# Both half-step FFNs of a decoder trunk: the gate/up products of the last two steps side by side, three down products behind them, and every step's rows turned by DMA

## The reference, cut to what matters

```python
def swiglu(x, w_gate, w_up, w_down):
    return (jax.nn.silu(x @ w_gate) * (x @ w_up)) @ w_down

def reference(x, ...):
    for l in range(DEPTH):                                     # DEPTH = 2
        x = x + HALF_STEP * swiglu(rmsnorm(x, norm_ffn1[l]), w1_gate[l], w1_up[l], w1_down[l])
        h = rmsnorm(x, norm_mix[l])
        proj = h @ w_in[l]
        ...                        # differential attention and retention on proj
        x = x + mixed @ w_out[l]
        x = x + HALF_STEP * swiglu(rmsnorm(x, norm_ffn2[l]), w2_gate[l], w2_up[l], w2_down[l])
    return rmsnorm(x, norm_final)
```

## Time and profile before

| | us |
|---|---|
| median of 3 runs | 959.06 (958.98 to 961.36) |
| the profiled execution | 961.72 |
| its span, first to last instruction | 959.6 |
| PE busy | 948.7 (99%) |
| DVE / ACT / POOL busy | 557.2 / 459.6 / 203.0 |
| mean granted PE clock | 0.996 of full speed |

### The profile page before, as it was taken

One profiled execution on the slowest core, in us unless ns is written; L12 is line 12 of the kernel. 1 busy time (PEld: TensorE's weight loads), 2 busy tenths in 40 slices (PEclk: granted clock), 3 DMA queues, 4 the chain that ended last, 5 costly groups with the idle time before them and its releaser, 6 DMA issues.

```text
span 959.6 us, 12597 instructions
## 1 busy us (share of the span) xinstructions
PE 948.7 (99%) x4379; PEld 785.6 (82%) x4379; DVE 557.2 (58%) x623; ACT 459.6 (48%) x580; POOL 203.0 (21%) x237
## 2 busy tenths in 40 slices
PE   8999999999999999999999999999999999999997
PEld 7888888888888888888888888888888887888885
DVE  5555555666575555555666455556665756555554
ACT  6454444455564454444445444444657445444442
POOL 4433221000010442131023221210002024312110
PEclk9999999999999999999999999999999999999999
DMA  7788676735353877676737767664624647867651
GB/s 266 237 219 251 185 226 196 247 121 170 113 187 121 230 230 232 190 229 194 246 117 216 242 196 228 189 220 150 228 80 176 219 119 207 266 191 220 195 161 44
DMA packets 166051, 185.98 MB, mean 194 GB/s; under 512 B 49264, under 2 KB 139424, under 8 KB 166016
## 3 DMA queue, kind: packets, MB, share of 16 engines
q1 hardware_dynamic: 122080, 174.09, 54.8%
q10 hardware_dynamic: 43616, 10.52, 6.2%
q0 software_dynamic: 320, 0.92, 0.6%
HBM read 173.96 MB, written 1.05 MB: 182 GB/s over the span
## 4 chain that ended last, share of the span: by engine, by line
PE 95%; DVE 1%; ACT 1%; DMA 1%; POOL 1%; issue 0%; POOLq 0%; DVEq 0%; ACTq 0%
PE gu L871 20%; PE gu L873 20%; PE gu L872 20%; PE acc L871 10%; PE acc L873 10%; PE acc L872 10%; PE tp L889 1%; PE tp L1007 1%; DMA kT<-kT 1%; PE acc L1018 1%; PE tp L1030 1%; ACT w_hi L360 1%; DVE w_lo L596 0%; PE gu L1119 0%; ACT rT L397 0%
## 5 line engine op out<-in xcount | busy, mean ns | idle before, releaser
L596 DVE TENSOR_TENSOR w_lo<-raw,w_hi 128x2048 fp32r<-128x2048 f32 (+1 forms) x164 | 374.3, 2286 | 157.7 <-ACT w_hi L360 157.7
L871 PE MATMUL gu<-w_hi,xT_hi 128*128 128x512 f32 x892 | 350.4, 393 | 1.2 <-DVE w_lo L605 1.0
L873 PE MATMUL gu<-w_hi,xT_lo 128*128 128x512 f32 x892 | 347.9, 390 | 0.0
L872 PE MATMUL gu<-w_lo,xT_hi 128*128 128x512 f32 x892 | 347.4, 390 | 0.0
L360 ACT ACTIVATE w_hi<-raw 128x2048 fp32r<-128x2048 f32 (+1 forms) x164 | 305.5, 1866 | 14.5 <-DMA raw<-in_w_in_dram 7.2
L871 PEld LDWEIGHTS gu<-w_hi,xT_hi 128*128 128x128 f32 x892 | 167.7, 188 | 37.0 <-DVE w_lo L605 1.4
L873 PEld LDWEIGHTS gu<-w_hi,xT_lo 128*128 128x128 f32 x892 | 167.6, 188 | 35.3
L872 PEld LDWEIGHTS gu<-w_lo,xT_hi 128*128 128x128 f32 x892 | 167.7, 188 | 33.6
L871 PE MATMUL acc<-w_hi,aT_hi 128*128 128x512 f32 x384 | 150.8, 393 | 0.7 <-DVE aT_lo L625 0.7
L873 PE MATMUL acc<-w_hi,aT_lo 128*128 128x512 f32 x384 | 149.7, 390 | 0.0
L872 PE MATMUL acc<-w_lo,aT_hi 128*128 128x512 f32 x384 | 149.5, 389 | 0.0
(11 more groups left out here) (129 smaller groups left out, 433.6 us busy)
## 6 DMA issues: line engine op xcount, KB each, us to landing
raw<-in_w_down_dram SPq DMA_DIRECT2D x88, 512.0 KB, 4.1
raw<-in_w_gate_dram SPq DMA_DIRECT2D x84, 512.0 KB, 4.0
raw<-in_w_up_dram SPq DMA_DIRECT2D x84, 512.0 KB, 5.0
raw<-in_w_in_dram SPq DMA_DIRECT2D x40, 512.0 KB, 4.7
raw<-in_w_out_dram SPq DMA_DIRECT2D x16, 512.0 KB, 4.1
raw<-in_w_in_dram SPq DMA_DIRECT2D x16, 256.0 KB, 3.0
raw<-in_w_gate_dram SPq DMA_DIRECT2D x8, 256.0 KB, 4.0
raw<-in_w_up_dram SPq DMA_DIRECT2D x8, 256.0 KB, 4.6
```

What stands on the lines that cost most here:

```text
L596: nc.vector.tensor_tensor(w_lo[:, pos % SLOTS, 0:n], raw[:, pos % RAW, 0:n], w_hi[:, pos % SLOTS, 0:n].bitcast(F32), ALU.subtract).then_in ...
L871: nc.tensor.matmul(out_, s_hi, m_hi, start=first, stop=False)
L872: nc.tensor.matmul(out_, s_hi, m_lo, start=False, stop=False)
L873: return nc.tensor.matmul(out_, s_lo, m_hi, start=False, stop=last)
```

## The change

The last two steps change places with their down products. PE now does, behind the loop: gate/up of step 8; down of step 7; gate/up of step 9; gate/up of step 10; down of step 8; down of step 9, tile 0; down of step 10, tile 0; down of step 9, tile 1; `enter_T`; down of step 10, tile 1. The 16 transposes of hidden rows on PE are gone, step 10 is turned by DMA like the others. The loop has one round less (steps 2 to 7), steps 8 and 9 are written out. Since aT_hi and aT_lo hold two steps, step 10 overwrites what step 8 left: ACT waits for PE's down of step 8, tile 0 (`aT_read`) and tile 1 (`slot_free`) first. The splits of pieces 33 and 34 stand each one place later. SP loads the pieces in PE's new order.

```diff
-LOOPED = (STEPS - 3) // 2
+LOOPED = (STEPS - 5) // 2
...
# SP
-                e = FFN_PIECES - 4
-                load_gu(0, e, STEPS - 1)
-                load_down(0, e + 2, STEPS - 2)
-                load_down(0, e + 3, STEPS - 1)
+                e = FFN_PIECES - 10
+                load_gu(0, e, STEPS - 3)
+                load_down(0, e + 2, STEPS - 4)
+                load_gu(0, e + 3, STEPS - 2)
+                load_gu(0, e + 5, STEPS - 1)
+                for n in range(3):
+                    load_down(0, e + 7 + n, STEPS - 3 + n)
...
# POOL
-                with pool.Fori(1 if i else 5, STEPS - 1) as s_:
-                    step(2 * s_ + d0, 2 * s_ + e0)
+                with pool.Fori(1 if i else 5, STEPS) as s_:
+                    step(2 * s_ + e0, 2 * s_ + e0)
...
# ACT
-                def last_step(s_, par, it, pos, nxt):
-
-                    silu(s_, 0, it, pos)
+                def last_step(s_, d, par, pos, nxt):
+
+                    silu(s_, 0, 0, pos)
                     nxt(0)
-                    silu(s_, 1, it, pos)
-                    last_hi(par, 0)
+                    turn(d, 0)
+                    silu(s_, 1, 0, pos)
+                    turn(d + 1, 1)
+                    act.wait_ge(aT_read, i + 1)
+                    turned_hi(d, par, 0)
                     nxt(1)
-                    last_hi(par, 1)
+                    act.wait_ge(slot_free, SLOTS + LP * layer + base + FFN_PIECES - 2)
+                    turned_hi(d + 1, par, 1)
+                    nxt(2)
...
                 def last_lots(i):
                     if i == 0:
                         split_hi(layer, base + FFN_PIECES - 1)
-                        ahead_after(layer, f, [0])
-                    elif i == 1:
-                        ahead_after(layer, f, [1])
+                    else:
+                        ahead_after(layer, f, [i - 1])
...
-                last_step(s0 + STEPS - 1, 0, 0, FFN_PIECES - 3, last_lots)
+                e, s = FFN_PIECES - 10, STEPS - 3
+                step(s0 + s, d0 + 2 * s, 0, 0, e + 1, pieces(0, e + 3, e + 4, e + 5))
+                split_hi(layer, base + e + 6)
+                step(s0 + s + 1, d0 + 2 * s + 2, 1, 0, e + 4, pieces(0, None, e + 7, e + 8))
+                last_step(s0 + s + 2, d0 + 2 * s + 4, 0, e + 6, last_lots)
...
# DVE, last_step (last_lots and the calls change as on ACT)
                     hide(e, 0, d - 1)
                     nxt(0)
                     hide(e + 1, 1, d)
-                    last_lo(par, 0)
+                    turned_lo(d, par, 0)
                     nxt(1)
-                    last_lo(par, 1)
+                    turned_lo(d + 1, par, 1)
+                    nxt(2)
...
# PE
-                for tt in range(TT):
-                    if tt == 0:
-                        hidden_T(e, 0)
-                    down((dT_lo_done, d0 + 2 * (STEPS - 1) - 1 + tt), 0, p_ + 2, 1, tt)
-                    if tt == 0:
-                        hidden_T(e + 1, 1)
-                    if tt and f == 0:
...
+                for s in (1, 2):
+                    for tt in range(TT):
+                        up(e0 + n + 2 * s + tt, 0, p_ + 1 + 2 * s, tt)
+                down((dT_lo_done, d0 + n + 1), 0, p_ + 7, 0, 0).then_inc(aT_read, 1)
+                down((dT_lo_done, d0 + n + 2), 0, p_ + 7, 0, 1)
+                for tt in range(TT):
+                    down((dT_lo_done, d0 + n + 3 + tt), 0, p_ + 8, 1, tt)
+                    if tt and (f == 0 or layer < DEPTH - 1):
                         enter_T(q + 1, 0)
-                    down((hT_lo_done, 2 * i + tt + 1), 0, p_ + 3, 0, tt, last=True)
+                    down((dT_lo_done, d0 + n + 5 + tt), 0, p_ + 9, 0, tt, last=True)
```

More of the change, by code:

```diff
@@ L141, in build @@
         rstd_tmp, normed = sem("rstd_tmp"), sem("normed")
-        gu_ready, silu_done, hidden_done, hT_psum, hT_hi_done, hT_lo_done = (
-            sem(n) for n in ("gu_ready", "silu_done", "hidden_done", "hT_psum", "hT_hi_done", "hT_lo_done"))
+        gu_ready, silu_done, hidden_done, aT_read = (sem(n) for n in ("gu_ready", "silu_done", "hidden_done", "aT_read"))
         pool_seen, halves_seen = sem("pool_seen"), sem("halves_seen")
@@ L674, in turned_lo @@
                           aT_hi[:, ks, tt * P:(tt + 1) * P], dT_lo_done)
[L676 to L680, removed]
                 def step(e, d, par, it, nxt, guard=True):
@@ L717, in ffn @@
                         step(e0 + 4 * it + 4 + 2 * u, d0 + 4 * it + 4 + 2 * u, u, it, pieces(it, p_, p_ + 1, p_ + 2))
-                last_step(e0 + 2 * (STEPS - 1), d0 + 2 * (STEPS - 1), 0, last_lots)
+                e, n = FFN_PIECES - 10, 2 * (STEPS - 3)
+                step(e0 + n, d0 + n, 0, 0, pieces(0, e + 3, e + 4, e + 5))
+                split_lo(layer, base + e + 6)
+                step(e0 + n + 2, d0 + n + 2, 1, 0, pieces(0, None, e + 7, e + 8))
+                last_step(e0 + n + 4, d0 + n + 4, 0, last_lots)
             def mixer(layer):
@@ L954, in up @@
                     project(layer, it, tt, base + pos, 2, gu_ready, hook, entry, entry is not None and base == 0)
[L956 to L960, removed]
                 def down(ready, it, pos, par, tt, **kw):
                     pe.wait_ge(*ready)
-                    add_rows(layer, it, tt, base + pos, aT_hi, aT_lo, 2 * par, **kw)
+                    return add_rows(layer, it, tt, base + pos, aT_hi, aT_lo, 2 * par, **kw)
                 up(e0, 0, 0, 0, lambda: enter_T(q, 1), guard=False, entry=q)
@@ L978, in ffn @@
                             down((dT_lo_done, d0 + n - 1 + tt), it, 7 + 3 * u, 1 - u, tt)
-                e, p_ = e0 + 2 * (STEPS - 1), FFN_PIECES - 4
+                n, p_ = 2 * (STEPS - 3), FFN_PIECES - 10
                 for tt in range(TT):
-                    up(e + tt, 0, p_, tt)
+                    up(e0 + n + tt, 0, p_, tt)
                 for tt in range(TT):
-                    if tt == 0:
-                        hidden_T(e, 0)
-                    down((dT_lo_done, d0 + 2 * (STEPS - 1) - 1 + tt), 0, p_ + 2, 1, tt)
-                    if tt == 0:
-                        hidden_T(e + 1, 1)
-                    if tt and f == 0:
+                    down((dT_lo_done, d0 + n - 1 + tt), 0, p_ + 2, 1, tt)
+                for s in (1, 2):
[6 more added lines that the diff above has]
+                    if tt and (f == 0 or layer < DEPTH - 1):
                         enter_T(q + 1, 0)
-                    elif tt:
-                        if layer < DEPTH - 1:
-                            enter_T(q + 1, 0)
-                    down((hT_lo_done, 2 * i + tt + 1), 0, p_ + 3, 0, tt, last=True)
+                    down((dT_lo_done, d0 + n + 5 + tt), 0, p_ + 9, 0, tt, last=True)
             def mixer(layer):
```

15 lines of the change are left out of this document (6 added, 9 removed).

## The result

The changed kernel takes 969.11 us (median of 6 runs, 967.39 to 971.0) against 960.2 us for the kernel before in 6 runs beside it (958.98 to 961.36). The ratio is 1.0096, 95% interval 1.0086 to 1.0106: slower by 9.2 us, where 5.7 were forecast. The time lies inside the range of 958.0 to 969.5, at its upper edge, and 0.1 us above the 962.1 to 969 of the forecast case; the amount is 1.6 times what was forecast. The profiled execution took 969.58 us, its span is 967.8 us, 8.2 more than before.

A forecast was written before the change was run, and what follows sets the result against it. PE, busy 948.7 of 959.6 us, was taken to bound the kernel. Three ends waiting 2.6 us (7.8) less 2.1 us saved at four ends gave +5.7 us: 964.8 us, range 958.0 to 969.5.

The forecast's parts named there:

- the forecast case: PE waits 1.7 to 4.0 us at three FFN ends, giving 962.1 to 969 us; chance 0.57.
- a wait of 2.6 us an end: PE's two waits at each of three FFN ends: 0.8 us before the down block, 1.8 before enter_T.
- x: Time from issue of step 10's first turn to its copy back: taken as 6.7 us, with ends 2.56 and 8.1.
- the fall of the clock: Rival: PE's gaps slow one down block after the waits, 2.9 us an end, 973 or so; 0.11 shared with the second hold-up.
- The gain: Two pairs of transposes per FFN leave PE: 0.52 us an end, 2.1 us over four ends.
- The held copy: POOL's copy of step 10's first hidden rows takes 2.50 us beside DVE's w_lo; turn issued 2.85 us after w_lo began.
- the row of 7.20: Before's turn at the second FFN's start, issue to copy back, two loads issued 3.0 and 0.4 us earlier: 7.20 us.
- The row of 7.93: Before's turn at the same place in layer 1: 7.93 us to landing alone, so about 8.1 to the copy back.
- The clock on which step 10 was laid: Before's timeline reused for the new order: PE starts step 10's row tile 1 at 171.87, DVE w_lo of piece 31 at 172.03.
- The formula: Both PE waits together at an FFN end: x - 4.1 us, nothing below x = 4.1.
- The hidden turn: Rival: step 10's first turn is hidden after all, deciding at x = 5.8; 956.9 to 960.2 us; hidden or nearly so 0.28.
- The second hold-up: Rival: step 9's tile 1 copy back held beside w_lo, 2.72 us, +6 us more, 970 or so; 0.11 shared with the clock.

The follow-up runs named there:

- the kernel without transposes: Kernel before with the stand-in, PE's 16 transposes of hidden rows left out: ratio 1.0004 to the kernel before.
- the stand-in: Each DMA turn replaced by a plain DMA of the same 128 KB, rows not turned: 1.0029 in before, 1.0084 in after, both to the kernel before.
- The longer path: Changed kernel with the stand-in, plus six ACT copies ahead of aT_hi at three FFN ends (path 1.9 us longer): ratio 1.0109 to the kernel before.
- light loads: Changed kernel with the stand-in, loads near these turns cut to 16 partitions of one tile: ratio 1.0002 to the kernel before.

## Why the prediction was wrong in size and right in cause

In short: the sum took a wait of 2.6 us an end, and 3.3 us were measured. The term that was sized too low is x, taken as 6.7 us where the three turns took 7.2 on average. Beside it the sum put two things at nothing, a longer hold of ACT's queue (0.9 us at one end) and the fall of the clock (1.1 us at one end), and one later stretch was counted 0.9 us too long.

- **The gain** (-0.52 us an end): right. 0.54 in the five blocks, 2.4 us by the kernel without transposes.
- **The held copy** (2.50 us, issue 2.85 us after w_lo begins): right, 175.96 to 178.81 is 2.85 us. Taking w_lo away from it, with the stand-in, ends all the waits at the ends, so its part is shown for the stand-in; for the real turn the rows fit the same account.
- **x = 6.7 us: the step that failed.** It measured 6.24, 7.92 and 7.50, mean 7.2, which at three ends is 1.6 us more in sum. I had put the turn nearest to the row of 7.20 and then drawn off half a us for a first load that was further along. The row of 7.93 in layer 1 was the better guide for two of three ends. x does depend on the loads: 2.5 us with light ones, 7.3 with whole ones, at the same place.
- **The clock on which step 10 was laid.** PE reached the five blocks at 177.39, forecast 177.31. But the path does not start with PE: the turn of step 9's second tile held ACT's queue 2.13 us and not 1.21, so w_lo of piece 31 began at 173.02 and not 172.03. About 0.9 us at the first end. I had assumed the usual duration of before for an instruction that everything behind it waits for; before itself has one issue of 2.39 us (at 65.15). What makes such an issue long stays open.
- **The fall of the clock** was a rival that would take the forecast's place, with 2.9 us an end. It came on top of the forecast case, at one end of three. Its net price is small: the residual adds began at 483.26 and enter_T could have followed 0.74 us later, as it does at the other ends (193.04 to 193.78), at 484.0; it came at 485.07. That is 1.1 us; the slow matmuls otherwise ran in time in which PE would have waited for DVE.
- **One term was too high**: at the end of layer 0 aT_lo to the residual adds takes 5.83 us (477.43 to 483.26) and not 6.68 as at the first end (186.36 to 193.04), since the next stage's pieces are split there in halves of 1024 and DVE begins the first half's w_lo while ACT splits the second (0.95 us after aT_lo and not 1.80), and the small copy is missing there. This is 0.9 us less.
- **The formula** (wait = x - 4.1) gives 2.1, 3.8 and 3.4 for the measured x. With the late issue (+0.9), the shorter path (-0.9) and the clock (+1.1) it is 3.0, 4.0 and 3.4; measured were 2.8, 4.0 and 3.1. So it holds within 0.3 us an end. The terms of the excess over 7.8 are +1.6 +0.9 -0.9 +1.1 -0.6 (rest) = 2.1 us.
- **The sum**: 9.9 us of loss at three ends less 2.2 for four ends' transposes is 7.8. The wait of the earlier trace rows in layer 1's second FFN did not recur (-0.9 us, which nothing of the change explains and I had not forecast), and 1.3 us are spread over the other stretches, 0.8 of it between the second and the third end. Named pieces of it are the waits for w_lo L601, 0.5 us against 0.2, and enter_T: at the two ends where it waited, it is 1.01 us to the next matmul (193.78 to 194.79) and not 0.79 as in before. The rest stays open. Together 8.2, the difference of the spans. The ratio of the runs says 9.2: two single executions are not the median of six.
- **The hidden turn** needed x under 5.8; the lowest of the three was 6.24. **The second hold-up** occurred only with the stand-in, and its price was wrong: it did not add to the first hold-up but took its place, since w_lo of piece 32 then began after the copy of step 10 was over.
- **The longer path** was to cost 5.7 us; the ends show 6.4, of which 3.6 at the two ends that can be compared, where 3.8 were expected; the ratios show 2.0. The expectation also took the clock to fall where a wait passes about 2 us: it fell after 1.89 and not after 2.88.

## What to carry to other kernels

When a step is made to depend on a transfer that other transfers run beside, price it with the slowest row of the same surroundings, not with a mean; and ask where the issue stands in its engine's order, since 1.9 us lost behind one DVE instruction can decide whether PE waits for a turn: here it also moved the turn among more loads. Here it paid to put the split of the next stage's pieces ahead of the instruction that waits for the transfer, and not behind it: the wait before enter_T went. Compare such changes by a stretch with a fixed number of matmuls and no idle time of its own: where nothing waits, 60 matmuls repeated within 0.02 us from kernel to kernel, while the stretch ahead of them varied by 4. With waits they vary too: after with the stand-in, profiled twice, gave 15.69 and 15.28 us at the middle end.

## What the runs showed of the hardware

- One DMA turn of 128 KB in the changed kernel: 2.4 us from issue to landing with no load beside it, 6.1 to 7.8 beside loads of 512 KB. The plain DMA of the same bytes, from issue to copy back: 2.5 us beside light loads, 3.9 to 7.3 beside whole ones.
- The issue of a DMA turn holds ACT's queue 1.21 us, once 2.13 (in before once 2.39); that of the plain DMA 0.60.
- A POOL copy of 128x512 that starts 0.25 us after a w_lo on DVE (128x2048, two inputs, 2.28 us) takes 2.50 us; with no w_lo beside it, 0.61.
- A gap of PE alone does not decide on the clock. It fell to 1.2 GHz after waits of 2.15 us (after) and 1.89 us (longer path, first end), and stayed at 2.4 GHz after 2.88 us and 1.88 us (longer path, other ends) and after 1.46 and 1.13 us. The granted clock was 0.72 of full speed over 476 to 482 us in the one, 0.64 over 187 to 190 us in the other, and seven to eight matmuls came at a pitch of 0.43 us. What decides is not shown.
- A wait costs PE some 0.25 us more than its length: at the first end the listed waits are 1.13 + 1.17 = 2.30 us and the loss is 2.79. The first matmul after a wait shows 0.51 us and not 0.39. Behind a wait the eight transposes of enter_T show 1.25 us and not 1.03.
